# A hybrid attention, SSD and MoE layer: parameter transfers, eps and the dt columns moved at the beginning

## What is computed

```python
h = rms_norm(x, mix_norm_w)
proj = h @ w_in
q, k, v, z, xbc, dt_raw, gate_a, gate_s = jnp.split(proj, IN_SPLITS, axis=-1)
lam = exp(sum(lambda_q1 * lambda_k1)) - exp(sum(lambda_q2 * lambda_k2)) + lambda_init
y_attn = diff_attention(q, k, v, lam, da_head_norm_w, lambda_init)   # 8 heads, each attn = probs[0] - lam * probs[1]
dt = softplus(dt_raw + dt_bias); a = -exp(a_log)                     # 32 columns of proj
y_ssd = ssd_mixer(z, xbc, dt, conv_w, conv_b, a, d_skip, ssd_norm_w)
x = x + (sigmoid(gate_a) * (y_attn @ w_attn_branch) + sigmoid(gate_s) * (y_ssd @ w_ssd_branch)) @ w_out
x = x + moe_ffn(rms_norm(x, moe_norm_w), ...)                        # 32 experts, top 4
x = x + sigmoid(rms_norm(x, ple_norm_w) @ w_ple_gate) * (p @ w_ple_proj)
y = rms_norm(x, final_norm_w)
```

## Time and profile before

| what | us |
|---|---|
| median of 3 runs | 2220.71 |
| lowest and highest | 2218.61, 2221.10 |
| the profiled execution, its own time | 2220.22 |
| span of the profile | 2218.4 |
| PE busy in the span | 2095.7 (94%) |
| DVE busy | 1613.7 (73%) |
| ACT busy | 1250.1 (56%) |
| share of PE in the chain that ended last | 89% |

### The profile page before, as it was taken

The page is one execution under the profiler, slowest core; times in us unless marked ns, Lnnn a source line. Parts: engine busy times, 40 slices in busy tenths (PEclk is TensorE's granted clock), DMA queues, the critical chain, the costliest instruction groups (busy, mean ns, idle before and its releaser), DMA issues.

```text
span 2218.4 us, 30507 instructions
## 1 busy us (share of the span) xinstructions
PE 2095.7 (94%) x9482; PEld 1613.2 (73%) x9482; DVE 1613.7 (73%) x1783; ACT 1250.1 (56%) x1426; POOL 122.2 (6%) x130
## 2 busy tenths in 40 slices
PE   6999999999699999869999999999999999999968
PEld 4777788888445554457888888888888888888846
DVE  4766878877611110368999999999999999999955
ACT  3444345345201010127888888888888888888844
POOL 2000011011000000000000100000000000000021
PEclk9999999999799999969999999999999999999989
DMA  7222222221043311278999999999999999999672
GB/s 252 75 71 73 67 77 61 71 66 48 22 139 95 90 52 31 91 289 327 392 380 386 386 386 386 382 390 376 392 383 389 385 385 386 376 393 379 246 247 98
DMA packets 244195, 528.08 MB, mean 238 GB/s; under 512 B 19565, under 2 KB 128182, under 8 KB 244150
## 3 DMA queue, kind: packets, MB, share of 16 engines
q1 hardware_dynamic: 228496, 474.93, 58.7%
q0 software_dynamic: 6912, 25.17, 3.5%
q10 hardware_dynamic: 8742, 27.40, 3.1%
HBM read 498.01 MB, written 29.43 MB: 238 GB/s over the span
## 4 chain that ended last, share of the span: by engine, by line
PE 89%; DVE 5%; DMA 2%; ACT 2%; issue 1%; SPq 0%; ACTq 0%; DVEq 0%; POOLq 0%
PE psum L1711 84%; PE psum L2014 1%; PE psum L2022 1%; DMA arena<-in_w_in 1%; DMA arena<-in_w_ple_proj 1%; DVE arena L1237 1%; DVE residual L1653 0%; PE psum L1886 0%; PE psum L1778 0%; DVE arena L1144 0%; DVE w_lo L1119 0%; PE psum L1846 0%; DVE arena L1455 0%; DVE arena L1454 0%; ACT arena L744 0%
## 5 line engine op out<-in xcount | busy, mean ns | idle before, releaser
L1584 DVE TENSOR_TENSOR h_lo<-arena,h_hi 128x1024 fp32r<-128x1024 f32 x768 | 909.2, 1222 | 94.5 <-ACT h_hi L1006 58.0
L1006 ACT ACTIVATE h_hi<-arena 128x1024 fp32r<-128x1024 f32 x768 | 804.9, 1060 | 209.1 <-PE psum L1711 190.6
L1711 PE MATMUL psum<-h_hi,w_hi 128*128 128x512 f32 x2176 | 866.0, 398 | 7.5 <-DVE w_lo L1119 2.8
L1711 PE MATMUL psum<-h_hi,w_lo 128*128 128x512 f32 x2176 | 850.4, 391 | 0.0
L1711 PE MATMUL psum<-h_lo,w_hi 128*128 128x512 f32 x2176 | 850.0, 391 | 0.0
L1711 PEld LDWEIGHTS psum<-h_hi,w_hi 128*128 128x128 f32 x2176 | 410.1, 188 | 103.7 <-issue 9.4
L1711 PEld LDWEIGHTS psum<-h_hi,w_lo 128*128 128x128 f32 x2176 | 409.7, 188 | 87.0
L1711 PEld LDWEIGHTS psum<-h_lo,w_hi 128*128 128x128 f32 x2176 | 410.4, 189 | 84.8 <-issue 3.8
L1711 PE MATMUL psum<-arena 128*128 128x512 f32 (+8 forms) x1264 | 365.6, 459 | 50.1 <-DVE arena L1455 13.4
L1711 PEld LDWEIGHTS psum<-arena 128*128 128x128 f32 (+1 forms) x1264 | 195.1, 201 | 206.1 <-issue 164.1
L1119 DVE TENSOR_TENSOR w_lo<-arena,w_hi 128x1024 fp32r<-128x1024 f32 x80 | 106.1, 1329 | 111.2 <-ACT w_hi L760 110.2
(11 more groups left out here) (271 smaller groups left out, 1424.4 us busy)
## 6 DMA issues: line engine op xcount, KB each, us to landing
arena<-in_w_up SPq DMA_DIRECT2D x512, 512.0 KB, 7.8
arena<-in_w_down SPq DMA_DIRECT2D x256, 512.0 KB, 7.0
arena<-in_w_in SPq DMA_DIRECT2D x80, 512.0 KB, 3.9
y_dram<-arena ACTq DMA_DIRECT2D x32, 512.0 KB, 8.9
arena<-in_w_ssd_branch SPq DMA_DIRECT2D x8, 1024.0 KB, 5.6
y_dram<-arena ACTq DMA_DIRECT2D x1, 7680.0 KB, 24.9
arena<-in_w_attn_branch SPq DMA_DIRECT2D x8, 512.0 KB, 3.8
arena<-in_w_out SPq DMA_DIRECT2D x2, 2048.0 KB, 13.7
```

The source lines that it names most:

```text
L1006: act.activation(piece_hi[slot], rows, ACT.Copy).then_inc(piece_hi_ready, 1)
L1584: dve.tensor_tensor(piece_lo[slot], rows, piece_hi[slot].bitcast(F32), ALU.subtract).then_inc(piece_lo_ready, 1)
L1711: return pe.matmul(o, l, r, start=start, stop=stop)
```

## The change

It does five things in the first 60 us, and nothing behind them.

1. `eps` is set by VectorE as its first instruction and has a semaphore of its own, so ScalarE's first root waits for that and not for GpSimd's last constant.
2. ScalarE's twelve parameter transfers come behind its splits of unit 0, unit 1 and the dt columns, ahead of the bias transfers and of the write of zeros.
3. SP loads the dt columns behind unit 0 and unit 1; ScalarE and VectorE split them behind these two.
4. TensorE multiplies the dt columns behind unit 1, into bank 2, and turns the parameters behind that. It turns the dt columns behind unit 2.
5. VectorE takes the dt columns and the parameters behind `split` of unit 3, and `ask_dt` and `finish_dt` come behind `split` of unit 4, directly ahead of the scores of head 0. ScalarE's exponentials for them come behind its copy of v.

```diff
-        dtT = vT[0:SH]
+        dtT = at(SCAN_AT, SEQ, extra=14 * SEQ)[0:SH]
@@ SP
-            sp.dma_start(w_dt, w_in_d[:, :, DT_AT:DT_AT + SH]).then_inc(w_dt_landed, 16)
...
+                        if isinstance(reg, int) and 2 * reg + h0 == 0 and j == 2:
+                            sp.dma_start(w_dt, w_in_d[:, :, DT_AT:DT_AT + SH]).then_inc(w_dt_landed, 16)
                         load_unit(attention_unit(j, h0, reg), reg * (2 * P) + (start + P * h0))
@@ GpSimd
-            pool.memset(eps[:], EPS)
@@ ScalarE
-            (the twelve parameter transfers)
-            act.wait_ge(consts_ready, 1)
+            act.wait_ge(eps_ready, 1)
...
             split_h(TT - 1)
+            split(Unit(0))
+            split(Unit(1))
             act.wait_ge(w_dt_landed, 16)
             act.activation(wdt_hi[:], w_dt, ACT.Copy).then_inc(wdt_split, 1)
-            split(Unit(0))
-            split(Unit(1))
+            (the twelve parameter transfers)
...
-                if first:
-                    act.wait_ge(lam_asked, 1)
-                    act.activation(lam[:, 2:4], lam[:, 0:2], ACT.Exp).then_inc(lam_exp_ready, 1)
-                    own.mark(act.activation(byhead[:, 1, :], byhead[:, 1, :], ACT.Exp))
-                    act.wait_ge(dt_exp_asked, 1)
-                    act.activation(dt_work[:, 2, :], dt_work[:, 1, :], ACT.Exp).then_inc(dt_exp_ready, 1)
...
                     act.activation(vT, bank(6), ACT.Copy).then_inc(vt_copied, 1)
+                    if first:
+                        (the same five lines)
@@ VectorE
+            dve.memset(eps[:], EPS).then_inc(eps_ready, 1)
...
-                if first:
-                    ask_dt()
                 split(attention_unit(2, h0, reg))
-                if first:
-                    finish_dt()
                 dve.wait_ge(unit_used, attention_unit(1, h0, reg).number + 1)
                 dve.tensor_copy(kT, bank(1)).then_inc(k_copied, 1)
                 split(attention_unit(3, h0, reg))
+                if first:
+                    dve.wait_ge(dt_projected, 1)
+                    dve.tensor_copy(dtT, bank(2)[0:SH]).then_inc(dtt_copied, 1)
+                    take_params()
                 split(attention_unit(4, h0, reg))
+                if first:
+                    ask_dt()
+                    finish_dt()
```

More of the change, by code:

```diff
@@ L799, in attention @@
                     act.activation(vT, bank(6), ACT.Copy).then_inc(vt_copied, 1)
+                    if first:
+                        act.wait_ge(lam_asked, 1)
+                        act.activation(lam[:, 2:4], lam[:, 0:2], ACT.Exp).then_inc(lam_exp_ready, 1)
+                        own.mark(act.activation(byhead[:, 1, :], byhead[:, 1, :], ACT.Exp))
+                        act.wait_ge(dt_exp_asked, 1)
+                        act.activation(dt_work[:, 2, :], dt_work[:, 1, :], ACT.Exp).then_inc(dt_exp_ready, 1)
                     act.wait_ge(v_turned, h + 1)
@@ L1165, in _, with take_params @@
             split_h(TT - 1)
+            split(Unit(0))
+            split(Unit(1))
             dve.wait_ge(wdt_split, 1)
             dve.tensor_tensor(wdt_lo[:], w_dt, wdt_hi[:].bitcast(F32), ALU.subtract).then_inc(wdt_split, 1)
-            split(Unit(0))
-            split(Unit(1))
-            dve.wait_ge(dt_projected, 1)
-            dve.tensor_copy(dtT, bank(6)[0:SH]).then_inc(dtt_copied, 1)
-            dve.wait_ge(params_turned, 1)
-            dve.tensor_copy(par[:], bank(7, NORMS))
-            own.then(dve.tensor_copy(conv_col[:].rearrange("p k t -> p (k t)"), bank(7, TAPS * CONV_TILES, P)))
-            own.then(dve.tensor_scalar(par_head, par_head, 1.0 - LAMBDA_INIT, None, ALU.mult))
-            for m in range(2):
-                ins = dve.tensor_tensor_reduce(out=lam_tmp[:, m, :], in0=lambdas[:, 2 * m, :],
-                                               in1=lambdas[:, 2 * m + 1, :], scale=1.0, scalar=0.0, op0=ALU.mult,
-                                               op1=ALU.add, accum_out=lam[:, m:m + 1])
-            ins.then_inc(lam_asked, 1)
             w = [dt_work[:, i, :] for i in range(8)]
             byh = lambda i: byhead[:, i, :].unsqueeze(1).broadcast_to([P, TT, SH])
+            def take_params():
+                dve.wait_ge(params_turned, 1)
+                dve.tensor_copy(par[:], bank(7, NORMS))
+                own.then(dve.tensor_copy(conv_col[:].rearrange("p k t -> p (k t)"), bank(7, TAPS * CONV_TILES, P)))
+                own.then(dve.tensor_scalar(par_head, par_head, 1.0 - LAMBDA_INIT, None, ALU.mult))
+                for m in range(2):
+                    ins = dve.tensor_tensor_reduce(out=lam_tmp[:, m, :], in0=lambdas[:, 2 * m, :],
+                                                   in1=lambdas[:, 2 * m + 1, :], scale=1.0, scalar=0.0, op0=ALU.mult,
+                                                   op1=ALU.add, accum_out=lam[:, m:m + 1])
+                ins.then_inc(lam_asked, 1)
             def ask_dt():
@@ L1766, in attention @@
                     project_unit(bank(0), attention_unit(0, h0, reg))
+                    project_unit(bank(1), attention_unit(1, h0, reg))
                     if first:
[L1768 to L1772 removed]
+                        project_dt()
                 if not first:
@@ L1785, in attention @@
                     project_unit(bank(6), attention_unit(2, h0, reg))
+                    if first:
+                        pe.wait_ge(dtt_copied, 1)
+                        for t in range(TT):
+                            ins = pe.transpose(bank(3, SH, t * SH), dtT[:, t * P:(t + 1) * P], ident[0:SH, 0:SH])
+                        ins.then_inc(dt_projected, 1)
                 if not first:
```

48 lines of the change are left out of this document (22 added, 26 removed).

## The result

| what | before | after |
|---|---|---|
| median of 12 runs each, us | 2220.95 | 2226.69 |
| lowest and highest | 2218.61, 2223.21 | 2225.49, 2228.60 |
| the profiled execution, its own time | 2220.22 | 2227.99 |
| span of the profile | 2218.4 | 2226.2 |
| idle time of TensorE ahead of the turning of v, head 0 | 1.78 | 5.86 |

The changed kernel takes 1.0028 times as long, interval 1.0020 to 1.0036. That is 5.7 us by the medians and 6.2 by the ratio. The prediction was 2225.6. I read the mechanism from the first 110 us, and the size of the whole from the medians.

The account below looks back on a forecast made before the run. From 56.86 us the kernel was taken as bound by TensorE, so the first head's shift reaches the end. Terms -4.2 + 5.9 + 1.6 + 1.7 = +5.0, with handovers +5.4, gave 2225.6 us, own range 2224 to 2228.

Parts of the forecast that it names:

- The start of the norm: Kernel start: without twelve issues ahead the norm starts earlier, taken as 2.9 us, the last `h_lo` ending at 21.3.
- End of unit 2, -4.2: TensorE, dt columns behind unit 1: unit 2 ends at 47.6 instead of 51.8, 4.2 us earlier.
- No wait of ScalarE for unit 2: ScalarE's split of unit 2: the load was taken to be in time, needed near 31.5, so no wait there.
- Unit 4, +1.6: Load of unit 4 beside the write of zeros: lands at 49.3 though wanted at 47.7, 1.6 us later.
- finish_dt, +5.9: Between unit 2 and head 0's first scores: 9.1 us in a row in place of 3.2, 5.9 us later.
- The table load: ScalarE ahead of the exponentials: taken as 1.28 us from the trace, without the skill page's drain of about 1.38 us.
- The transfer's share of the engines: Unit 4's load beside the write: 520 packets against 723 by the trace, preferred to equal turns, estimated at 11.7 us.
- The clock, +1.7: TensorE, last two score steps and start of unit 3: run at the lower clock level, costing 1.7 us.
- Handovers, 0.2 to 0.5: More numerous handovers were to add 0.2 to 0.5 us to the sum of the terms.
- Unit 3 at 63.3: TensorE: unit 3 was to start near 63.3 where it started at 57.92.
- The transfer is in time: Rival, chance 0.36: unit 4 lands before 47.7, the sum is +3.2 to +3.8, time 2223.7.
- The parameters clog the queue: Rival, chance 0.15: small transfers delay unit 3, unit 4 lands near 54, 6 us late; time 2229.9.

Follow-up runs that it names:

- e2_zeros_late: The changed kernel with the write of zeros issued behind ScalarE's split of unit 4 instead of behind the bias transfers; 2223.25 us, 1.0012 times before.
- e5_busy_gap: The changed kernel with 24 unread matmuls on TensorE ahead of the turning of v and 15 ahead of head 0's third score step; 2227.61 us.
- e10_busy_second_gap: The changed kernel with 24 unread matmuls only ahead of the third step of head 0's scores; 2226.86 us, 1.0028 times before.
- e11_busy_gap_again: The same kernel as `e5_busy_gap`, run a second time for a second trace; 2224.32 us, 1.0012 times before.
- e4_early_norm: The kernel before with only eps set by VectorE and the twelve parameter transfers behind the first splits; 2228.55 us, 1.0031 times before.
- e1_covered: The changed kernel with dt columns turned ahead of unit 2, exponentials, ask_dt and finish_dt ahead of the splits of unit 4; 2219.45 us, 0.9991 times before.
- e9_transfers_first: The changed kernel with the twelve parameter transfers first again on ScalarE's queue, ahead of the norm; 2227.84 us, 1.0039 times before.
- e3_both: `e1_covered` with the write of zeros moved behind ScalarE's split of unit 4; 2218.74 us, 0.9990 times before.
- e8_covered_zeros_540: `e1_covered` with the write of zeros issued at about 541 us; 2216.85 us, 0.9988 times before.
- e6_before_zeros_540: The kernel before with only the write of zeros moved, to about 541 us; 2218.53 us, 0.9991 times before.

## Why the prediction was right, and where it was off

The predicted time was 1.1 us below the measured one, and the side and the mechanism were right. That it came so close is in part luck: unit 4 was 1.7 us short, four other terms were too large by 0.9 us together, and unit 0, which I took as fixed, differs by over 1 us between executions. Slower by more than 0.2% had 0.50; the measured ratio is 1.0028, its interval begins at 1.0020. By its own steps:

- **The start of the norm: right.** First multiplication 6.75 (6.6 predicted), last `h_lo` ending at 21.24 (21.3), first product at 22.52 (22.5). The first square came at 3.99, sooner than my 4.5, and nothing hung on it. Tile 1 landed at 7.92 (8.0). The timeline of VectorE, of after:

```profile
6.75 1.28 DVE L1143 SCALAR_TENSOR_TENSOR arena<-residual,stat,arena 128x1024 f32<-128x1024 f32 x1 [0.88 <-DMA arena<-in_mix_norm_w]
```

- **End of unit 2, -4.2: right,** measured -4.4. In `e2_zeros_late`, `e5_busy_gap`, `e10_busy_second_gap` and `e11_busy_gap_again`, in which nothing that TensorE waits for up to there was changed, unit 2 ends at 46.6, 46.4, 47.3 and 48.0 where after has 47.4, so this term is known to 0.6 to 1.0 us either way. The parameters, issued from 18.97 to 27.3, were hidden; `e4_early_norm` shows that this cover was worth 5.6 us, and that I was right to ask what it costs if it goes, but had written no number for it.
- **"No wait of ScalarE for unit 2": wrong.** It waits 0.91 us, until 32.04. TensorE doesn't notice, since it wants unit 2 at 41.7. But SP loads unit 4 behind that split, so this is where the next term went off.
- **Unit 4, +1.6: the mis-sized term,** measured +3.3. I had 33.3 for the issue and 49.3 for the landing, so 16.0 us of transfer; it took 16.30. The duration taken from the earlier trace rows was right. The issue came at 34.39, 1.1 us later than I had it, because I let unit 2 be in time on ScalarE and it was not; 0.3 more come from the duration, and 0.3 from TensorE being done earlier, so that unit 4 was wanted at 47.4 and not at 47.7. The step that failed is "I therefore let unit 2 be in time": I held that against TensorE's need and not against SP's next load.
- **finish_dt, +5.9: right,** measured +5.8. From the landing to the first scores there are 8.9 us (9.1 predicted). `e1_covered` takes the term out: 5.6. The timeline of after has `finish_dt` from 53.80 to 59.70 where I had 52 to 58, later by unit 4's error.
- **The table load.** The exponential stands 0.01 us behind the end of the load (52.27 + 1.28, then 53.56), in after as in the earlier trace rows. The 1.38 us of drain that the Trainium skill ("ScalarE: Activation LUTs", section "What ACT_TABLE_LOAD costs") counts on top show nowhere in these chains, and a sum with them would have been off by that much.
- **The transfer's share of the engines: the duration was right, the reading behind it was not.** In us 36 to 44 of after q1 moves 531 packets beside 737 of q10, against 520 and 723 in the earlier trace rows, and I took this for a lower share of q1. But both stretches begin before the load's first packet. In after, unit 4 is issued at 34.39, q1 moves nothing from 35 to 37, and its packets begin at 37.8. The queues of after in us 35 to 37, and then in us 39 to 49:

```profile
q10 hardware_dynamic: 267, 0.83, 103.6%
...
q10 hardware_dynamic: 894, 3.66, 88.8%
q1 hardware_dynamic: 895, 0.46, 15.1%
```

From then on the two queues move as many packets as each other, 90 per us, and 1024 rows need 11.4 us. Before, unit 2 is issued at 25.71, its packets begin at 29.9, and from 31 to 45 q1 moves 1249 and q10 1248. Turns of one packet each, as the Trainium skill has it ("DMA: Bandwidth & Descriptors", section "Queues, rings and completion order"), gave an estimate of 11.7 us; the trace agrees for the time in which the load's packets move. What that estimate left out is the 3.4 us from the issue to the first packet, and the rest up to the landing. So unit 4 landed at 50.7 and not at the 45 to 47 of that estimate.

- **The clock, +1.7: right in the trace,** 1.0 until unit 3 and 0.6 in it. For the whole time I can't say it was shown.
- **Handovers, 0.2 to 0.5: not there.** The account closes without them.
- **Unit 3 at 63.3: measured 63.57.** The sum of the trace is +6.25 where I wrote +5.4, and the difference is +1.7 of unit 4, less 0.2 at unit 2, 0.1 at `finish_dt`, 0.1 at the clock and 0.4 of handovers. The medians give +5.7.
- **The rivals.** "The transfer is in time", to which I had given 0.36, was not so: 3.3 us late. `e2_zeros_late` is that case made: +2.2 by the medians and +2.7 by the ratio, where I had +3.5; still no change that could be told. "The parameters clog the queue" did not come: unit 3 took 11.1 us and was in near 34.7, just when the write began to move and 3 us ahead of unit 4's first packet, and unit 4 landed at 50.7, not at 54. "The start gives more" would have needed unit 2 to end 5.9 us earlier; 4.4 was all. "The norm doesn't start earlier" is the start of `e9_transfers_first`, +7.9 by the medians where I had +7.3, though by another mix of terms, since there TensorE waits for unit 2 and not for unit 4.

## What to carry to other kernels

When a step is moved earlier behind a single long transfer, ask not only whether its own load is in time for the bottleneck engine, but when its split releases the load after next: in after, before and `e9_transfers_first` the long write hits a load that is waited for, and the shift chooses which; in `e2_zeros_late` and with the write at 541 us it hits none that is waited for. Work of a side engine that lies beside a busy bottleneck engine is free; the same work between two of its steps costs its whole length (5.92 us of VectorE cost 5.6 to 5.8). Of a change made of several moves, find the one that needs another as its cover: the early norm alone was a loss of some 7 us, and with the dt product behind unit 1, `finish_dt` covered and the write moved a gain of some 3.

## What the runs showed of the hardware that I had not expected

- **A 512 KB load of 512-byte rows beside a long write takes three to four times as long.** Alone it had 4.9 us. Beside the write it had 17.9 and 16.30 in after, 11.65 in `e4_early_norm`, where part of the write was over. Two things add up: the first packets come 3.4 us (after), 4.2 us (before) and 4.3 us (unit 6 of `e2_zeros_late`) behind the issue, where unit 7 of `e2_zeros_late`, all but alone, has 1.0; then the load and the write move as many packets as each other, 90 per us. Unit 2 took 9.61 with only unit 3 and the small parameter transfers beside it, also where the write was gone (`e2_zeros_late`).
- **A queue can back up.** Of the twelve parameter issues on ScalarE's queue ten take 0.30 to 0.52 us and the last two 1.50 and 2.15; ScalarE's own work runs on beside them. A transfer of 32 KB from the end of that row landed 9.3 us behind its issue (`e4_early_norm`).
- **The same idle time, another clock.** In four kernels TensorE idles 1.78 us ahead of the turning of v, which takes 0.63 in each. From the first scores to unit 3 they then take 2.95 (before), 3.37 (`e3_both`), 3.36 (`e8_covered_zeros_540`) and 3.90 us (`e6_before_zeros_540`). With 3.31 and 4.76 us of idle time `e1_covered` and `e4_early_norm` took 3.00 and 3.17. After, `e2_zeros_late` and `e9_transfers_first`, with 5.86, 2.63 and 2.63 and a second idle time of 3.98 ahead of the third step of scores, took 3.95, 3.95 and 3.94. The length of the last idle time alone does not say which level follows.
- **Single executions of one kernel lie several us apart,** from 2.3 us between the lowest and the highest (`e11_busy_gap_again`) to 9.6 (`e3_both`), and the parts of the chain show where. One place is unit 0, which takes 7.2 to 8.6 us in the kernels that begin as after does. Behind the first head the shift of a pair is constant to 0.2 us up to 540 us and then moves (after, from 6.1 to 7.7 at 600 us; `e8_covered_zeros_540`, from -3.8 to -2.0 at 564 us, -3.3 at 578 us and -2.9 by 770 us), in the stages in which the granted clock moves. So of two traces the first 110 us can be compared to some tenths only from a common point on, such as the end of unit 2; across unit 0 they differ by up to 1.4 us, and their spans can't be compared.
